# Stick-breaking attention in a fused transformer kernel: later key blocks added up on VectorE ahead of the matmuls with minus ones

## The reference, cut to what matters

```
mask = kpos[None, :] < qpos[:, None]
z = einsum('bhqd,bhkd->bhqk', qi, k) * scale
log_nb = where(mask, log_sigmoid(-z), 0.0)
after = cumsum(log_nb, axis=3, reverse=True) - log_nb
w = where(mask, exp(log_sigmoid(z) + after), 0.0)
out = einsum('bhqk,bhkd->bhqd', w, v)
```

## Time and profile before

| | |
|---|---|
| median of 3 runs | 2866.57 us (2865.85 to 2868.82) |
| the profiled execution | 2866.88 us, of it span 2865.2 us |
| TensorE busy (matmuls) | 2807.3 us, 98% of the span |
| VectorE busy | 1457.5 us, 51% |
| ScalarE busy | 984.2 us, 34% |
| the stick-breaking rounds | from about 1338 to 1555 us of the span |
| matmuls of line 2106 | 320, 20 for each of 16 heads |

### The profile page before, as it was taken

How to read it: one execution, slowest core, us unless ns; L and a number is a source line. 1 busy time by engine, 2 the same in 40 slices (tenths; PEclk the granted TensorE clock), 3 DMA queues, 4 the chain that set the end, 5 groups by cost and what they waited for, 6 DMA issues and landing times. The chain is left out here.

```text
span 2865.2 us, 34079 instructions
## 1 busy us (share of the span) xinstructions
PE 2807.3 (98%) x13630; PEld 2326.4 (81%) x13630; DVE 1457.5 (51%) x1931; ACT 984.2 (34%) x1093; POOL 32.9 (1%) x68
## 2 busy tenths in 40 slices
PE   7999999999999999999999999999999899899998
PEld 6888887788888888888887888888888788788886
DVE  7774356467743677434444443435545543623333
ACT  4222237432222322224444322324434432422221
POOL 0000000000000000000000000000000000000000
PEclk9999999999999999999999999999999999999999
DMA  5332231134322343222121322224311122222222
GB/s 182 136 139 88 103 134 60 45 134 148 136 103 103 125 140 138 95 107 92 49 74 45 118 89 102 88 103 147 110 70 65 45 74 103 74 102 92 98 103 74
DMA packets 68128, 288.80 MB, mean 101 GB/s; under 512 B 9488, under 2 KB 30352, under 8 KB 38464
## 3 DMA queue, kind: packets, MB, share of 16 engines
q1 hardware_dynamic: 59520, 257.97, 25.6%
q0 software_dynamic: 7936, 29.23, 3.0%
q10 hardware_dynamic: 576, 0.23, 0.0%
HBM read 285.31 MB, written 2.10 MB: 100 GB/s over the span
## 5 line engine op out<-in xcount | busy, mean ns | idle before, releaser
L1019 DVE TENSOR_TENSOR sb_WL<-sb_RAW,sb_WH 128x2048 fp32r<-128x2048 f32 x242 | 554.4, 2291 | 762.1 <-ACT sb_WH L435 761.9
L1797 PE MATMUL PS<-sb_HH,sb_WH 128*128 128x512 f32 x2288 | 900.8, 394 | 13.1 <-DVE sb_HL L1035 9.2
L1798 PE MATMUL PS<-sb_HL,sb_WH 128*128 128x512 f32 x2288 | 892.7, 390 | 0.0
L1799 PE MATMUL PS<-sb_HH,sb_WL 128*128 128x512 f32 x2288 | 892.6, 390 | 0.0
L435 ACT ACTIVATE sb_WH<-sb_RAW 128x2048 fp32r<-128x2048 f32 x242 | 463.2, 1914 | 788.5 <-PE PS L1799 786.6
L1797 PEld LDWEIGHTS PS<-sb_HH,sb_WH 128*128 128x128 f32 x2288 | 431.2, 188 | 107.9 <-issue 18.7
L1798 PEld LDWEIGHTS PS<-sb_HL,sb_WH 128*128 128x128 f32 x2288 | 431.1, 188 | 91.5 <-issue 3.4
L1799 PEld LDWEIGHTS PS<-sb_HH,sb_WL 128*128 128x128 f32 x2288 | 430.9, 188 | 90.5
L1797 PE MATMUL PS<-ff_GH,sb_WH 128*128 128x512 f32 x880 | 342.5, 389 | 1.9 <-DVE sb_WL L1019 1.9
L1798 PE MATMUL PS<-ff_GL,sb_WH 128*128 128x512 f32 x880 | 342.4, 389 | 0.0
L1799 PE MATMUL PS<-ff_GH,sb_WL 128*128 128x512 f32 x880 | 342.4, 389 | 0.0
(11 more groups left out here) (350 smaller groups left out, 2544.8 us busy)
## 6 DMA issues: line engine op xcount, KB each, us to landing
sb_RAW<-in_weights SPq DMA_DIRECT2D x230, 1024.0 KB, 4.8
ff_ADAW<-in_w_ada POOLq DMA_DIRECT2D x48, 512.0 KB, 4.0
sb_RAW<-in_weights SPq DMA_DIRECT2D x22, 512.0 KB, 5.1
sb_XT<-in_x SPq DMA_DIRECT2D x4, 512.0 KB, 9.7
out_t<-sb_XT SPq DMA_DIRECT2D x4, 512.0 KB, 2.7
b_CT<-in_ctx POOLq DMA_DIRECT2D x1, 1024.0 KB, 5.3
sb_RAW<-in_weights SPq DMA_DIRECT2D x4, 256.0 KB, 4.3
hy_BD<-in_c_gates POOLq DMA_DIRECT2D x1, 512.0 KB, 3.3
```

The source lines that it names most:

```text
L1019: dve.tensor_tensor(WL[slot][:, :], RAW[slot][:, :], f32(WH[slot][:, :]), ALU.subtract).then_inc(*T["w_lo"].up())
L1797: pe.matmul(out, wh, xh, start=start, stop=False)
L1798: pe.matmul(out, wh, xl, start=False, stop=False)
L1799: return pe.matmul(out, wl, xh, start=False, stop=stop)
```

## The change

VectorE now also makes, for each head, the sums of later blocks. After SL it adds block 3 onto the columns of block 2 that have the same queries (128 columns), and the result onto block 1 (256 columns), in place in E. Block 1's 384 columns of E then hold the sum of the blocks 1 to 3, and the last 256 columns hold the sum of blocks 2 and 3 with their queries. Both are split into a high part AH (cast) and a low part AL (subtraction), each 384 + 256 columns. The last of these raises a new semaphore, `sb_al`. TensorE makes all four pairs with TRI first, waits for `sb_al`, and makes three pairs with NONE: block 0 takes AH/AL of blocks 1 to 3, block 1 those of 2 and 3, and block 2 takes SH/SL of block 3 as before. ScalarE's first pass waits for `sb_al` of two heads before in place of `sb_sl`, since E is in use until then. AL lies where SQT and HT lie, which the stage doesn't use.

```
 # ScalarE, sb_logs
                 if h >= 2:
-                    act.wait_ge(T["sb_sl"].sem, h - 1)
+                    act.wait_ge(T["sb_al"].sem, h - 1)
 # VectorE, sb_soft
                 dve.tensor_tensor(sbm["SL"][:, h % 2, :], E, f32(sbm["SH"][:, h % 2, :]), ALU.subtract).then_inc(*T["sb_sl"].up())
+                dve.wait_ge(*T["sb_sl"].now())
+                for i, w in ((2, P), (1, 2 * P)):
+                    later = E[:, OFF[i + 1]:OFF[i + 1] + w]
+                    step(dve.tensor_tensor(E[:, OFF[i] + P:OFF[i] + P + w], E[:, OFF[i] + P:OFF[i] + P + w], later, ALU.add))
+                parts = [(E[:, o:o + w], sbm["AH"][:, h % 2, a:a + w], SBAL[:, h % 2, a:a + w]) for o, w, a in ((512, 384, 0), (1024, 256, 384))]
+                for src, hi, _ in parts:
+                    last = dve.tensor_copy(hi, src)
+                step(last)
+                for src, hi, lo in parts:
+                    last = dve.tensor_tensor(lo, src, f32(hi), ALU.subtract)
+                last.then_inc(*T["sb_al"].up())
 # TensorE, sb_logs
                 pe.wait_ge(T["sb_sl"].sem, h + 1)
                 for i in range(TB):
-                    for j in range(i, TB):
-                        w = S - P * j
-                        o = OFF[i] + P * (j - i)
-                        for part in ("SH", "SL"):
-                            last = pe.matmul(zs(h)[:, o:o + w], sbm["TRI" if i == j else "NONE"][:, :], sbm[part][:, h % 2, OFF[j]:OFF[j] + w],
-                                             start=False, stop=True, skip_group_check=True)
+                    w = S - P * i
+                    for part in ("SH", "SL"):
+                        pe.matmul(zs(h)[:, OFF[i]:OFF[i] + w], sbm["TRI"][:, :], sbm[part][:, h % 2, OFF[i]:OFF[i] + w],
+                                  start=False, stop=True, skip_group_check=True)
+                pe.wait_ge(T["sb_al"].sem, h + 1)
+                for i in range(TB - 1):
+                    w, a = S - P * (i + 1), (0, 384)[i % 2]
+                    for later in ((sbm["AH"][:, h % 2, a:a + w], SBAL[:, h % 2, a:a + w]) if i < 2 else
+                                  [sbm[part][:, h % 2, OFF[3]:OFF[3] + P] for part in ("SH", "SL")]):
+                        last = pe.matmul(zs(h)[:, OFF[i] + P:OFF[i] + P + w], sbm["NONE"][:, :], later,
+                                         start=False, stop=True, skip_group_check=True)
                 last.then_inc(*T["sb_tri"].up())
```

More of the change, by code:

```diff
@@ L160, in build @@
         EPSC = sb("EPSC", [P, 1])
-        SQT, SSACC, RINV = sb("SQT", [P, 2, S]), sb("SSACC", [P, S]), sb("RINV", [P, S])
-        HT = sb("HT", [P, 2, S])
+        SBAL = layout("sba", [("AL", [P, 2, 640], F32R)])["AL"]
+        SQT, HT = sb("SQT", [P, 2, S]), sb("HT", [P, 2, S])
+        SSACC, RINV = sb("SSACC", [P, S]), sb("RINV", [P, S])
         SPT = sb("SPT", [P, 8, 12])
@@ L183, in build @@
                              ("SH", [P, 2, 1280], F32R), ("SL", [P, 2, 1280], F32R), ("W", [P, 2, 1280], F32), ("TRI", [P, P], F32R),
-                             ("NONE", [P, P], F32R), ("MASK", [P, P], F32R), ("EYE", [P, P], F32R)])
+                             ("NONE", [P, P], F32R), ("MASK", [P, P], F32R), ("EYE", [P, P], F32R),
+                             ("AH", [P, 2, 640], F32R)])
         hyy = layout("hyy", [("YH0", [P, 4, S], F32R), ("YH1", [P, 4, S], F32R), ("YL1", [P, 4, S], F32R), ("HOLE", [P, 4, S], F32),
@@ L230, in build @@
             "xc_ready", "rg_mm", "rg_sig", "rg_at", "rg_b2", "rg_sq", "y_f32", "y_hi", "y_ready", "up_clear",
-            "qk_sq", "qk_ss", "qk_rms", "qk_norm", "f_abs", "f_ln", "c_ready", "c_hi", "c_lo", "fx_const", "sb_const", "sb_sl", "sb_half", "sb_taken", "qk_in", "fx_half", "fx_taken",
+            "qk_sq", "qk_ss", "qk_rms", "qk_norm", "f_abs", "f_ln", "c_ready", "c_hi", "c_lo", "fx_const", "sb_const", "sb_al", "sb_sl", "sb_half", "sb_taken", "qk_in", "fx_half", "fx_taken",
             "fx_s", "fx_max", "fx_exp", "fx_p", "fx_t", "fx_pt", "fx_o",
```

## The result

| | before | after |
|---|---|---|
| median, us | 2868.10 (6 runs, the three of above among them) | 2875.41 (6 runs, 2874.80 to 2881.71) |
| profiled execution, us | 2866.88 | 2874.98 |
| TensorE busy, us | 2807.3 | 2803.5 |
| VectorE busy, us | 1457.5 | 1491.5 |

The changed kernel is slower: 7.3 us by the medians, 8.1 between the two profiled executions. The ratio over all runs, one of 2881.71 us among them, is 1.0033 (95% interval 1.0023 to 1.0043), which would be 9.5 us. The forecast was 3.5 us more. The measured median lies at the upper edge of the range, and the loss is more than twice what was forecast.

A forecast was written before the change was run, and what follows sets the result against it. TensorE was taken to bound the stage, with VectorE's chain deciding in every round. 0.98 + 3 x 1.07 - 3 x 1.12 + 2.63 = +3.5 us gave 2870.1 us, range 2866 to 2875.5.

The forecast's parts named there:

- What bounds the stage, and the margins: Stick-breaking rounds: TensorE busy 215.46 of 217.00 us; K's take has 4.58 us in hand in round 2, 3.64 in round 3.
- What TensorE saves: Sums of each head: three pairs fewer save 0.68 us a head, 10.9 us over 16 heads if nothing waited.
- The price by columns / 2.4 + 2.5 ns: Other estimate for the removed matmuls on TensorE: 442 ns a head, 7.1 us over 16 heads in place of 10.9.
- What VectorE pays: VectorE's list after SL: six added instructions cost 2.30 us more a head, 4.60 a round.
- Both slower rivals: On VectorE: narrow casts at additions' pace, 2875.3 us, chance 0.13; or short instructions not overlapping, 2874.1 us, chance 0.09.
- What costs nothing: ScalarE's wait for AL of two heads before, the exponentials, and later low weights and raw weight loads: no cost.
- Rounds 0, 1, 2, 4, 6: Per round: round 0 loses 0.98 us, round 1 loses 1.07, rounds 2, 4 and 6 gain 1.12 each.
- Rounds 3 and 5, and the last: Rounds 3 and 5 lose 1.07 us each waiting for K; the last loses 2.63 behind the odd head's late SL and AL.
- pays another 0.11: Restart price of a TensorE that had to wait: 0.11 us, the next matmul's start 0.34 away in place of 0.23.
- The reach of a shift: After the stage: nothing else changes and TensorE bounds both sides, so a shift of the stage's end reaches the program's end.

The follow-up runs named there:

- e2: Kernel before, TensorE's sums cut to seven pairs a head, VectorE adding nothing up: 2855.42 us, 0.9959 times before.
- e4: e3 with VectorE taking K out of PSUM right behind the odd head's AL, ahead of the output remainder: 2865.24 us, 0.9992 times before.
- e1: Changed kernel with TensorE's ten pairs a head put back and no wait for AL, VectorE's added work kept: 2876.26 us, 1.0033 times before.
- e7: Kernel before, with unread VectorE additions ahead of K's take in rounds 1 to 6 (10 in even rounds, 7 in odd): 1.0038 times before, +9.9 us.
- e3: Changed kernel with the V weights' high and low parts made at the start of rounds 1, 3 and 5: 2866.14 us, 0.9995 times before.
- e8: Kernel before, with unread VectorE additions ahead of K's take in rounds 1 to 6 (11 in even rounds, 8 in odd): 1.0055 times before, +16.2 us.
- e9: Kernel before, with unread VectorE additions ahead of K's take in rounds 1 to 6 (13 in even rounds, 10 in odd): 1.0123 times before, +35.3 us.

## Why the prediction was wrong

- **What bounds the stage, and the margins**: right. TensorE bound it, and the take of K, the odd head's SL and AL were the places where VectorE's longer list came through. In round 2 the V projection started at 1413.96, 0.05 behind the end of K's take, as counted.
- **What TensorE saves**: right. 0.69 us a head in e2, 0.68 forecast. The price by columns / 2.4 + 2.5 ns that the Trainium skill gives ("TensorE: Matmul & The Clock Gate", "Back-to-back issue gap") was too low. The same section says that this formula is for a matmul by itself and comes out short at few columns because it leaves out the weight load, and it gives about 81 ns a matmul of 128 columns in a stream; here a pair of them took 0.23 us.
- **What VectorE pays**: right, 2.31 us a head against 2.30. The narrow casts follow the wide one, and short instructions without a wait do overlap: the two remainders of 559 and 419 ns take 0.89 together. Both slower rivals fall. The time of one of them, 2875.3, is nearly the one measured, and that is luck: its cause is not there.
- **What costs nothing**: right. ScalarE's first pass waited for TensorE's scores, and no wait of ScalarE for AL shows.
- **Rounds 0, 1, 2, 4, 6**: right within 0.1 us.
- **Rounds 3 and 5, and the last**: wrong, and this is the step that failed. The prediction said of a TensorE that had to wait that it "pays another 0.11", and priced a loss as the idle time and that restart. It saw the idle time coming ("about 2.5 us in the odd" rounds) and asked nothing about the clock, which the busy table gave as full for the whole stage because TensorE never stood for more than 0.8 us there. Behind 2.35 us of idle time it fell in two of three rounds, which then took 1.5 us more than the third, and behind 2.77 in the last, 0.7. That is 3.7 us on top of what the VectorE list costs, of a miss of 4.05 in the stage. A fall of the clock would have been a rival of its own, at 3.5 + 4 x 1.5 = 9.5 us if it fell in all four long waits. What decides, behind an idle time of about 2 us, whether the clock falls stays open. The Trainium skill has the warning on that same page ("Why this matters for your kernels"): idle gaps between bursts of matmuls bring the lower clock back. The gap that it names is longer than the 2.35 us here, so by its letter these waits would have passed; the measurement decides.
- **The reach of a shift**: right in the main. By the medians the clock outside the stage makes a few tenths to 1.6 us of difference either way, and 2.7 in the profiled execution of e4.

## What to carry to other kernels

Moving work from the bounding engine to an engine that is half idle pays only if the second engine has time in hand at the very places where the first one waits for it; read that margin at each of them, round by round, and find room there (a 2.2 us instruction moved to the start of three rounds was worth 8.4 to 9.5 us here) before moving the work, or leave the move out in the rounds that have no room. Price a new wait on TensorE as the idle time and, from about 2 us on, as a stretch at half the clock behind it: here a wait of 1 us cost 1 us, and one of 2.35 us cost 2.4 or 3.8.

## What the runs showed of the hardware

- Idle times of TensorE of 0.97 and 1.3 to 1.4 us in the stage were never followed by a lower clock (9 cases in e1 and e7), nor were those of 1.15 us in round 0 of the changed kernel, e3 and e4, and of 1.49 in the last round of e2. Those of 1.9 us at about 1850 us were in 6 of 12 profiles, of 2.0 to 2.2 us in 2 of 6 cases (e8), of 2.35 us in 2 of 3 (the changed kernel), of 2.77 and 3.11 us in 4 of 4 (the last rounds of the changed kernel, e1, e3 and e4), of 3.5 to 3.6 us in 6 of 6 (e9). So two rounds with the same instructions can differ by 1.5 us in one execution.
- The clock can fall while TensorE still waits (e4, and e9, where 0.58 was granted in the last 2 us of the wait) or some time after it has begun again: 0.4 us in round 3 of the changed kernel, 1.2 us in the last round of e1.
- A matmul that follows one of 128 columns takes 0.05 us longer until the next starts: a pair of 384 columns 0.39 in place of 0.34 us, and the second matmul of 128 columns in a pair 0.11 where the first took 0.07. Their 128 columns alone would take 0.053 us at 2.4 GHz. No run shows why.
- A cast from float to fp32r is cheaper than an addition also at 256 and 384 columns: 286 and 360 ns, where the additions of rows 4 take 425 and 547. Two columns per 1.04 ns on top of 0.155 us would make 288 and 355.
